# Expert weights of a mixture-of-experts layer laid out by partition, one 3 MB load per expert

## The chip, the cores and the metric

The kernel runs on one core of one Trainium2 chip. The metric is the device time of one execution in microseconds (us): the median of three runs. All data is fp32.

## The reference, cut to what matters

One encoder layer over 768 tokens of 1024 features (a prompt of 256 tokens and a sample of 512). Attention of two kinds, an output projection and a residual come first. Then each token is normalised, goes to one group of experts and to the top two of the eight experts in it; there are 32 experts, each a gated MLP with 256 hidden features. The change lies in this last part:

```python
h = rmsnorm(x, ffn_norm)                      # (tokens, 1024)
gates = ...                                   # top-1 group, top-2 experts in it
for e in range(32):
    y = (silu(h @ w_gate[e]) * (h @ w_up[e])) @ w_down[e]   # 1024 -> 256 -> 1024
    out = out + gates[:, e:e+1] * y
return rmsnorm(x + out, final_norm)
```

Each of the three weights of an expert has 1 MB, so the experts read 96 MB from HBM in all.

## The kernel before, in words

The engines run programs of their own (blocks `sync`, `gpsimd`, `scalar`, `vector`, `tensor`) that meet at semaphores. Attention (up to about 370 us) and the output projection with the router (to about 477 us) come first.

**Routing.** For each of the six tiles of 128 tokens VectorE (DVE) computes the normalised rows `h2` (`ffn_norm`, L1259) and the experts; GpSimd (POOL) stores the rows to HBM (L723) and scatters the numbers of the token-expert pairs into a table by expert (`note_pairs`, L717). `h2` is written with its features permuted: word (c, p) of the row is feature p * 8 + c, because chunk c of the transposed rows has to meet the rows p * 8 + c of the weights.

**The expert stage.** An expert works on blocks of 64 rows; `extras` gives how many further blocks it has (8 over all experts here: experts 8, 9, 14, 15 and 19 have one and expert 13 has three). The 32 experts go in groups of six, with ring slot s for the s-th expert of a group. For each expert:

- SyncE (SP), `load_expert` (L538): three loads of 1 MB, `w_gate`, `w_up` (L557) and `w_down` (L561), into one ring slot of 6144 words a partition. From the second group on it first waits until the expert six before is done (`last_done`, L554), and each load is paced: it waits for the landing of the load three issues before it (`paced`, L550). `w_gate` and `w_up` lie in SBUF as (p, c, n): partition p holds the rows p * 8 + c, so that a partition reads 8 KB in one piece. The last expert's weights go into the place of the residual, early. After the last load SP reloads the residual (L595).
- GpSimd gathers the block's rows from HBM (`gather`, L739 and L741), four experts ahead; further blocks have one buffer, and the gather of the next one waits until TensorE has transposed the one before (`e_xeT_psum`). Results are scattered to HBM (L749, and L832 for the last four).
- TensorE (PE), `pe_group` (L1810): waits for gate and up of the expert; `gate_up` (L1758) is 8 chunks times two halves of the hidden features, the halves in the two column halves of the array, each product 256 columns wide (128 of gate, 128 of up). Half h takes the hidden features 2n + h, every second word of a weight row. Then the next expert's rows are transposed (L1754), then, after a wait for `w_down` (`down_weights`, L1805), the down products of the expert before (L1773), and the transposed hidden block (L1803). The trace has two records for each fp32 product: 32 for a `gate_up`.
- ScalarE (ACT) computes the silu (L1021) and copies the results out (L1029, L1037), DVE multiplies (L1401) and copies transposed blocks (L1406, L1424, L1411).

After the last expert the rows come back from HBM (L601, L603), are weighted and added to the residual on PE (L1869) and DVE (L1448 to L1458), and stored.

Two definitions that the prediction counts with:

```python
SLOT_W = 3 * D * FF // P        # 6144 words a partition, 3 MB a slot
ring = [arena[:, a:a + SLOT_W] for a in [QKV0 + s * SLOT_W for s in range(4)] + [R0, W0]]
```

Of the kernel before, what the change touches and what calls it, by code (L numbers as in the profile page):

```python
# [18 lines left out]
P = 128  # L19
# [120 lines left out]
def build(nc, A):  # L140
# [12 lines left out]
    with ExitStack() as ctx:  # L153
# [260 lines left out]
        last_loaded = sem("last_loaded")  # L414
        gate_loaded = [sem(f"gate_loaded{s}") for s in range(RING)]
        up_loaded = [sem(f"up_loaded{s}") for s in range(RING)]
        down_loaded = [sem(f"down_loaded{s}") for s in range(RING)]
        id_ready = sem("id_ready")
# [75 lines left out]
        def _(sp):  # L494
# [43 lines left out]
            def load_expert(g, s):  # L538


                e = g * RING + s
                w = weights(g, s)
                last = is_last(g, s)
                later = not isinstance(g, int) or g > 0 and not last

                def paced(what, slot, back):
                    if later:
                        turn = g + (slot - back) // RING + 1
                        sp.wait_ge(what[(slot - back) % RING], 16 * turn)
                        sp.sem_inc(waited, 1)  # L550

                if later:
                    sp.wait_ge(last_done, e - RING + 1)
                    sp.sem_inc(waited, 1)  # L554
                for i, (n, pace) in enumerate((("w_gate", (down_loaded, s, 2)), ("w_up", (gate_loaded, s, 1)))):
                    paced(*pace)
                    sp.dma_start(w[:, i * 2048:(i + 1) * 2048],  # L557
                                 A[n][0, bass.ds(e, 1), :, :].rearrange("o (p c) n -> p (o c n)", c=DC)
                                 ).then_inc(last_loaded if last else (gate_loaded, up_loaded)[i][s], 16)
                paced(up_loaded, s, 1)  # L560
                sp.dma_start(w[:, 4096:6144],  # L561
                             A["w_down"][0, bass.ds(e, 1), :, :].rearrange("o (p j) n -> p (o j n)", p=P)
                             ).then_inc(last_loaded if last else down_loaded[s], 16)

# [514 lines left out]
        def _(dve):  # L1079
# [171 lines left out]
            def ffn_norm(t):  # L1251
                dve.wait_ge(rms2_ready, t + 1)
                link(dve.reciprocal(rs[:, t:t + 1], rs[:, t:t + 1]))
                if t == 0:
                    dve.wait_ge(gffn_in, 16)
                if t >= 2:
                    dve.wait_ge(h2_stored[t % 2], 16 * (t // 2))

                dve.scalar_tensor_tensor(h2[t % 2].rearrange("n (c p) -> n c p", c=DC),  # L1259
                                         x_tok[:, t, :].rearrange("n (p c) -> n c p", c=DC), rs[:, t:t + 1],  # L1260
                                         gain_ffn.rearrange("n (p c) -> n c p", c=DC), ALU.mult, ALU.mult).then_inc(h2_ready, 1)

# [214 lines left out]
        def _(pe):  # L1477
# [280 lines left out]
            def gate_up(b, i, w):  # L1758


                w = w[:, 0:4096].rearrange("p (g c n h) -> p g c h n", g=2, c=DC, h=2)
                for c in range(DC):
                    for h in range(2):
                        last = nc.tensor.matmul(bank(b)[h * SLOTS:(h + 1) * SLOTS, 0:2 * P].rearrange("p (g n) -> p g n", g=2),  # L1764
                                                x_eT[i][:, c, :], w[:, :, c, h, :],
                                                start=(c == 0), stop=(c == DC - 1))
                return last
# [36 lines left out]

            def down_weights(g, s):  # L1805

                if not is_last(g, s):
                    await_count(down_loaded[s % RING], 16 * (g + s // RING + 1))

            def pe_group(g):  # L1810
                words = load_counts(pe, g)
                for s in members(g):
# [3 lines left out]
                    if is_last(g, s):  # L1816
                        pe.wait_ge(last_loaded, 48)
                    else:
                        pe.wait_ge(gate_loaded[s], 16 * (g + 1))
                        pe.wait_ge(up_loaded[s], 16 * (g + 1))  # L1820
                    pe.wait_ge(xeT_ready, e + 1)
# [3 lines left out]
                    if not isinstance(g, int) or e:  # L1825
                        down_weights(g, s - 1)
                        down_before(k, g, s - 1, last_done)
                    h_transpose(k)
                    with pe.If(n > 0):
                        down_weights(g, s)  # L1830
                        with pe.Fori(0, n) as j:
                            transpose_further(before + j)
                            pe.wait_ge(hT_ready, k + j + 1)
                            pe.wait_ge(y_out, k + j + 1)
                            down(weights(g, s), 0)
                            pe.wait_ge(e_xeT, before + j + 1)
                            gate_up(1, 2, weights(g, s)).then_inc(gu_done, 1)
                            down(weights(g, s), 1).then_inc(part_done, 1)
                            h_transpose(k + j + 1)
# [78 lines left out]
```

## Time and profile before

| | us |
|---|---|
| median of 3 runs (798.39, 800.14, 801.2) | 800.14 |
| the profiled execution | 800.14 |
| its span, first to last instruction | 798.4 |
| PE busy in it | 745.3 (93%) |
| DVE, ACT, POOL busy | 301.8, 220.0, 199.4 |
| moved by DMA | 154.64 MB, 203 GB/s of HBM traffic over the span |
| mean granted TensorE clock | 0.975 of 2.4 GHz |

The sum of busy times says little here, since attention, projection and expert stage have different limits; the rows below are by stretch. The profiled execution's time stands 1.7 us over its span. In the profile "released by issue" means that an engine waited for nothing that the trace shows. A busy PE need not be a fast PE: ends of matmuls are modelled.

### The profile page before, as it was taken

To read this page: it belongs to the slowest core of one execution; us is meant where nothing else is said; L and a number is where in the kernel's file an instruction comes from. 1 tells how busy PE (TensorE), PEld (TensorE's weight loads), DVE (VectorE), ACT (ScalarE), POOL (GpSimd) and SP (SyncE) were. 2 spreads that over 40 slices of the span, in tenths; PEclk is the share of its full clock that TensorE was granted. 3 is DMA by queue.
4 is the path that set the end of the run, shared out by engine and by line. 5 is a ranking of instruction groups with operands and counts; after the bars stand their busy time and mean duration, and the time that the engine had idled before them with its cause. 6 is when DMAs were issued, how large, how long until landed. Compare 5 with 4: busy or idle time off the path is not lost. (4 is left out here: it accounts for less than half of the span.)

```text
span 798.4 us, 12355 instructions
## 1 busy us (share of the span) xinstructions
PE 745.3 (93%) x4034; PEld 411.0 (51%) x4035; DVE 301.8 (38%) x811; ACT 220.0 (28%) x595; POOL 199.4 (25%) x479
## 2 busy tenths in 40 slices
PE   8999999999888999989999974999998999999995
PEld 4555554444355666664555552555544454545542
DVE  3442211010288888980555562111111121211126
ACT  3543220111277767660211110111110111111123
POOL 1233422210023232032001223441321434342110
PEclk9999999999999999999999986999998999999999
DMA  9603002000320000000891258899999999999948
GB/s 348 258 1 106 0 1 105 1 0 1 113 104 1 2 1 1 2 1 0 347 421 76 80 213 307 273 351 372 374 344 388 391 348 333 410 379 387 401 163 347
DMA packets 36887, 154.64 MB, mean 194 GB/s; under 512 B 9674, under 2 KB 10826, under 8 KB 23904
## 3 DMA queue, kind: packets, MB, share of 16 engines
q1 hardware_dynamic: 28112, 136.50, 44.9%
q0 software_dynamic: 7648, 15.75, 6.0%
q10 hardware_dynamic: 1072, 1.70, 0.6%
q8 instruction: 28, 0.46, 0.2%
q14 instruction: 27, 0.22, 0.1%
HBM read 142.29 MB, written 20.03 MB: 203 GB/s over the span
## 5 line engine op out<-in xcount | busy, mean ns | idle before, releaser
L1499 PE MATMUL banks<-arena 128*128 128x512 f32 (+1 forms) x384 | 163.7, 580 | 2.3 <-issue 1.9
L1764 PE MATMUL banks<-arena 128*64 128x256 f32 x1280 | 158.2, 399 | 4.6 <-issue 2.4
L1764 PEld LDWEIGHTS banks<-arena 128*64 128x64 f32 x1280 | 90.9, 138 | 63.9 <-issue 10.8
L1499 PEld LDWEIGHTS banks<-arena 128*128 128x128 f32 x384 | 72.1, 193 | 79.6 <-issue 79.6
L1655 PE MATMUL banks<-arena 128*128 128x512 f32 x192 | 86.4, 598 | 1.1 <-DVE arena L1237 1.1
L1773 PE MATMUL banks<-arena 128*64 128x512 f32 x320 | 79.8, 610 | 0.5 <-ACT arena L1029 0.5
L1401 DVE TENSOR_TENSOR arena<-arena,banks 128x128 f32<-128x128 f32 x40 | 11.6, 290 | 165.4 <-ACT arena L1021 165.4
L1193 DVE TENSOR_REDUCE arena<-banks 128x1 f32<-128x512 f32 (+1 forms) x96 | 55.3, 599 | 48.0 <-PE banks L1571 41.5
L952 ACT ACTIVATE arena<-banks,arena 128x512 f32<-128x512 f32 (+1 forms) x96 | 58.3, 613 | 42.4 <-DVE arena L1196 21.0
L1021 ACT ACTIVATE arena<-banks 128x128 f32<-128x128 f32 x40 | 11.1, 278 | 160.5 <-PE banks L1764 160.5
L1655 PEld LDWEIGHTS banks<-arena 128*128 128x128 f32 x192 | 35.2, 191 | 38.8 <-issue 37.4
L741 POOL DMA_INDIRECT arena<-h_rows,arena x40 | 39.1, 977 | 34.8 <-POOL arena L739 34.8
L881 ACT ACTIVATE arena<-banks,arena 128x512 f32<-128x512 f32 (+1 forms) x24 | 16.0, 666 | 106.5 <-PE banks L1499 106.5
L1606 PE MATMUL banks<-arena 128*128 128x128 f32 x240 | 36.1, 282 | 9.0 <-issue 5.5
L749 POOL DMA_INDIRECT pair_rows<-arena x36 | 36.5, 1013 | 31.8 <-POOL arena L747 30.6
L1754 PE MATMUL banks<-arena 64*128 64x64 f32 x320 | 29.1, 233 | 15.5 <-DMA arena<-h_rows,arena 15.4
L1606 PEld LDWEIGHTS banks<-arena 128*128 128x128 f32 x240 | 26.1, 142 | 31.3 <-issue 26.2
L1571 PE MATMUL banks<-arena 96*128 96x512 f32 (+1 forms) x96 | 40.1, 540 | 2.1 <-ACT arena L952 1.2
L480 POOL TENSOR_SCALAR arena<-arena 128x2 f32<-128x2 f32 (+1 forms) x8 | 1.6, 195 | 152.6 <-ACT arena L980 152.6
L1029 ACT ACTIVATE arena<-banks 128x512 f32<-128x512 f32 x32 | 19.1, 597 | 71.7 <-PE banks L1773 71.7
L1754 PEld LDWEIGHTS banks<-arena 64*128 64x128 f32 x320 | 23.7, 142 | 29.5 <-issue 18.3
L630 POOL TENSOR_TENSOR arena<-arena 128x64 f32<-128x64 f32 (+2 forms) x24 | 8.0, 331 | 117.8 <-ACT arena L881 67.8
(201 smaller groups left out, 880.6 us busy)
## 6 DMA issues: line engine op xcount, KB each, us to landing
arena<-w_gate SPq DMA_DIRECT2D x32, 1024.0 KB, 12.3
arena<-w_up SPq DMA_DIRECT2D x32, 1024.0 KB, 12.9
arena<-w_down SPq DMA_DIRECT2D x32, 1024.0 KB, 13.3
arena<-w_in SPq DMA_DIRECT2D x3, 2048.0 KB, 8.3
arena<-pair_rows SPq DMA_DIRECT2D x5, 1024.0 KB, 11.3
arena<-w_out SPq DMA_DIRECT2D x1, 4096.0 KB, 13.1
arena<-x SPq DMA_DIRECT2D x6, 512.0 KB, 10.6
h_rows<-arena POOLq DMA_DIRECT2D x6, 512.0 KB, 5.6
```

Of the source, the lines that this page charges most:

```text
L741: pool.indirect_dma_start(x_rows[i], None, h2_dram, bass.IndirectOffsetOnAxis(ap=id_cur[0:SLOTS, i:i + 1], axis=0), bounds_check=T - 1, oo ...
L749: pool.indirect_dma_start(y_dram, bass.IndirectOffsetOnAxis(ap=yid_cur[:, i:i + 1], axis=0), y_sb[i], None, bounds_check=4 * T - 1, oob_is ...
L952: act.activation(p_tok[u % 3][:, a, 0:nt * P], bank(2 * (u % 2) + a)[:, 0:nt * P], ACT.Exp, bias=nbias[:, u % 4, a:a + 1], scale=MLA_SCALE ...
L1029: act.activation(y_sb[s % YBUF], bank(4), ACT.Copy).then_inc(y_out, 1)
L1193: dve.reduce_max(mx[:, u % 4, a:a + 1], bank(2 * (u % 2) + a)[:, 0:nt * P], X_).then_inc(dve_chain, 1)
L1499: last = nc.tensor.matmul(bank(mm % 2)[:, 0:GROUP_COLS[g]], xgT[:, t, c, :], w[:, c, :], start=(c == 0), stop=(c == DC - 1))
L1571: nc.tensor.matmul(bank(2 * (u % 2) + a)[:, 0:nt * P], qT[0:QK, 2 * j + a, tok], kT[0:QK, 2 * j + a, keys], start=True, stop=True).then_in ...
L1606: last = nc.tensor.transpose(bank(4 + tau % 2)[:, kt * P:(kt + 1) * P], p_tok[u % 3][:, a, kt * P:(kt + 1) * P], ident)
L1655: last = nc.tensor.matmul(bank(2 * (t % 2) + h), aT[:, c, t * P:(t + 1) * P], w_out_sb[:, c, h * 512:(h + 1) * 512], start=(c == 0), stop= ...
L1754: last = nc.tensor.transpose(bank(b)[:, c * SLOTS:(c + 1) * SLOTS], x_rows[i][:, c * P:(c + 1) * P], ident[half, half])
L1764: last = nc.tensor.matmul(bank(b)[h * SLOTS:(h + 1) * SLOTS, 0:2 * P].rearrange("p (g n) -> p g n", g=2), x_eT[i][:, c, :], w[:, :, c, h, ...
L1773: last = nc.tensor.matmul(bank(4)[h * SLOTS:(h + 1) * SLOTS, :], h_T[:, j * SLOTS:(j + 1) * SLOTS], w[:, j, h * 512:(h + 1) * 512], start= ...
```

## The change

On the host the three weights of an expert are laid side by side by partition: partition p of `w_expert[e]` holds gate rows c * 128 + p for c = 0..7, then up rows likewise, then down rows j * 128 + p for j = 0, 1: 24 KB in one piece, 3 MB an expert. SP loads an expert with one DMA on one semaphore per slot, and each load waits for the landing of the expert's load two before it (and for its slot). PE waits for all three weights before `gate_up`, and the later waits for `w_down` are gone. The half h of the hidden features is now h * 128 + n, 128 adjacent words, and the rows `h2` are written in their natural order.

```diff
@@ -412,9 +412,7 @@
         waited = sem("waited")
 
         last_loaded = sem("last_loaded")
-        gate_loaded = [sem(f"gate_loaded{s}") for s in range(RING)]
-        up_loaded = [sem(f"up_loaded{s}") for s in range(RING)]
-        down_loaded = [sem(f"down_loaded{s}") for s in range(RING)]
+        weights_in = [sem(f"weights_in{s}") for s in range(RING)]
         id_ready = sem("id_ready")
         rows_in = [sem(f"rows_in{i}") for i in range(RING + 1)]
         xeT_psum = sem("xeT_psum")
@@ -543,24 +541,13 @@
                 last = is_last(g, s)
                 later = not isinstance(g, int) or g > 0 and not last
 
-                def paced(what, slot, back):
-                    if later:
-                        turn = g + (slot - back) // RING + 1
-                        sp.wait_ge(what[(slot - back) % RING], 16 * turn)
-                        sp.sem_inc(waited, 1)
-
                 if later:
                     sp.wait_ge(last_done, e - RING + 1)
                     sp.sem_inc(waited, 1)
-                for i, (n, pace) in enumerate((("w_gate", (down_loaded, s, 2)), ("w_up", (gate_loaded, s, 1)))):
-                    paced(*pace)
-                    sp.dma_start(w[:, i * 2048:(i + 1) * 2048],
-                                 A[n][0, bass.ds(e, 1), :, :].rearrange("o (p c) n -> p (o c n)", c=DC)
-                                 ).then_inc(last_loaded if last else (gate_loaded, up_loaded)[i][s], 16)
-                paced(up_loaded, s, 1)
-                sp.dma_start(w[:, 4096:6144],
-                             A["w_down"][0, bass.ds(e, 1), :, :].rearrange("o (p j) n -> p (o j n)", p=P)
-                             ).then_inc(last_loaded if last else down_loaded[s], 16)
+                    sp.wait_ge(weights_in[(s - 2) % RING], 16 * (g + (s - 2) // RING + 1))
+                    sp.sem_inc(waited, 1)
+                sp.dma_start(w, A["w_expert"][bass.ds(e, 1), :, :].rearrange("o p n -> p (o n)")
+                             ).then_inc(last_loaded if last else weights_in[s], 16)
 
             sp.wait_ge(pv_done, N_UNITS)
             for s in range(4):
@@ -1256,9 +1243,7 @@
                 if t >= 2:
                     dve.wait_ge(h2_stored[t % 2], 16 * (t // 2))
 
-                dve.scalar_tensor_tensor(h2[t % 2].rearrange("n (c p) -> n c p", c=DC),
-                                         x_tok[:, t, :].rearrange("n (p c) -> n c p", c=DC), rs[:, t:t + 1],
-                                         gain_ffn.rearrange("n (p c) -> n c p", c=DC), ALU.mult, ALU.mult).then_inc(h2_ready, 1)
+                dve.scalar_tensor_tensor(h2[t % 2], x_tok[:, t, :], rs[:, t:t + 1], gain_ffn, ALU.mult, ALU.mult).then_inc(h2_ready, 1)
 
             def first_max(key, values, rev, m):
 
@@ -1758,11 +1743,11 @@
             def gate_up(b, i, w):
 
 
-                w = w[:, 0:4096].rearrange("p (g c n h) -> p g c h n", g=2, c=DC, h=2)
+                w = w[:, 0:4096].rearrange("p (g c n) -> p g c n", g=2, c=DC)
                 for c in range(DC):
                     for h in range(2):
                         last = nc.tensor.matmul(bank(b)[h * SLOTS:(h + 1) * SLOTS, 0:2 * P].rearrange("p (g n) -> p g n", g=2),
-                                                x_eT[i][:, c, :], w[:, :, c, h, :],
+                                                x_eT[i][:, c, :], w[:, :, c, h * P:(h + 1) * P],
                                                 start=(c == 0), stop=(c == DC - 1))
                 return last
 
@@ -1801,11 +1786,6 @@
 
                 pe.wait_ge(h_ready, k + 1)
                 nc.tensor.transpose(bank(3)[:, 0:P], h_tok, ident).then_inc(hT_psum, 1)
-
-            def down_weights(g, s):
-
-                if not is_last(g, s):
-                    await_count(down_loaded[s % RING], 16 * (g + s // RING + 1))
 
             def pe_group(g):
                 words = load_counts(pe, g)
@@ -1814,20 +1794,17 @@
                     n, before = extras(words, s)
                     k = e + before
                     if is_last(g, s):
-                        pe.wait_ge(last_loaded, 48)
+                        pe.wait_ge(last_loaded, 16)
                     else:
-                        pe.wait_ge(gate_loaded[s], 16 * (g + 1))
-                        pe.wait_ge(up_loaded[s], 16 * (g + 1))
+                        pe.wait_ge(weights_in[s], 16 * (g + 1))
                     pe.wait_ge(xeT_ready, e + 1)
                     gate_up(1, s % 2, weights(g, s)).then_inc(gu_done, 1)
                     if not isinstance(g, int) or e + 1 < NE:
                         transpose_rows(g, s + 1)
                     if not isinstance(g, int) or e:
-                        down_weights(g, s - 1)
                         down_before(k, g, s - 1, last_done)
                     h_transpose(k)
                     with pe.If(n > 0):
-                        down_weights(g, s)
                         with pe.Fori(0, n) as j:
                             transpose_further(before + j)
                             pe.wait_ge(hT_ready, k + j + 1)
@@ -1909,6 +1886,13 @@
     for n in WEIGHTS:
         arrays[n] = np.ascontiguousarray(np.asarray(inputs[n]))
     arrays["w_in"] = arrays["w_in"].reshape(D, -1)
+
+    def by_partition(w):
+
+        return np.ascontiguousarray(w.reshape(NE, w.shape[1] // P, P, -1).transpose(0, 2, 1, 3).reshape(NE, P, -1))
+
+    arrays["w_expert"] = np.ascontiguousarray(np.concatenate(
+        [by_partition(arrays.pop(n)[0]) for n in ("w_gate", "w_up", "w_down")], axis=2))
     A = {n: nc.dram_tensor(n, a.shape, mybir.dt.from_np(a.dtype), kind="ExternalInput").ap() for n, a in arrays.items()}
     for n, s in (("y_prompt", S_PROMPT), ("y_sample", S_SAMPLE)):
         A[n] = nc.dram_tensor(n, (1, s, D), mybir.dt.float32, kind="ExternalOutput").ap()
```

## Rows read from the trace of the kernel before

**Rows 1.** The page, section 1: busy us (share of the span) and instructions.

```profile
PE 745.3 (93%) x4034; PEld 411.0 (51%) x4035; DVE 301.8 (38%) x811; ACT 220.0 (28%) x595; POOL 199.4 (25%) x479
```

**Rows 2.** Stretches: engines' busy us (records), granted clock, DMA share, GB/s.

```profile
390.00:418.00 28.00, 28.00 (x104) 15.46 (x103) 13.98 (x61) 5.01 (x14) 0.60 (x1) 1.00 1.01 422
...
531.00:592.00 61.00, 59.91 (x448) 30.62 (x450) 11.78 (x28) 8.47 (x19) 20.09 (x34) 1.00 1.02 368
...
592.00:645.00 53.00, 47.84 (x341) 25.12 (x337) 8.63 (x20) 5.54 (x14) 16.01 (x28) 0.94 1.02 373
...
665.00:748.00 83.00, 81.71 (x614) 43.08 (x616) 15.48 (x37) 10.73 (x25) 29.02 (x50) 1.00 1.01 385
```

**Rows 3.** Groups of the page: the gate and up products (busy us, mean ns).

```profile
L1764 PE MATMUL banks<-arena 128*64 128x256 f32 x1280 | 158.2, 399 | 4.6 <-issue 2.4
```

**Rows 4.** Timeline of PE: start us, length us, line; one attention burst, three expert bursts.

```profile
333.71 1.10 PE L1625 MATMUL banks<-arena 128*64 128x128 f32 x16
...
751.64 3.87 PE L1764 MATMUL banks<-arena 128*64 128x256 f32 x32
...
756.08 1.94 PE L1773 MATMUL banks<-arena 128*64 128x512 f32 x8
...
758.21 3.88 PE L1764 MATMUL banks<-arena 128*64 128x256 f32 x32
```

**Rows 5.** SP's waits between 480 and 770 us: us in total, times, longest.

```profile
SPq L550 <- DMA arena<-w_up: 57.8, 23, 3.9
...
SPq L550 <- DMA arena<-w_gate: 53.3, 19, 4.5
...
SPq L554 <- PE banks L1773: 47.1, 10, 11.1
```

**Rows 6.** Timeline of SP, 380 to 798 us: issues of expert loads.

```profile
578.34 0.33 SPq L561 DMA_DIRECT2D arena<-w_down  x1
...
658.33 0.33 SPq L557 DMA_DIRECT2D arena<-w_gate  x1
...
743.07 0.33 SPq L561 DMA_DIRECT2D arena<-w_down  x1
```

**Rows 7.** DMA issues between 573 and 580 us: median us to landing (one w_down).

```profile
arena<-w_down SPq DMA_DIRECT2D x1, 1024.0 KB, 14.3
```

**Rows 8.** Timeline of PE around experts 13 and 14.

```profile
591.44 3.88 PE L1764 MATMUL banks<-arena 128*64 128x256 f32 x32
...
608.08 1.08 PE L1754 MATMUL banks<-arena 64*128 64x64 f32 x8 [3.54 <-DMA arena<-h_rows,arena]
...
632.11 0.68 PE L1754 MATMUL banks<-arena 64*128 64x64 f32 x8 [1.41 <-DMA arena<-h_rows,arena]
```

**Rows 9.** DMA issues between 737.5 and 744 us (one w_down).

```profile
arena<-w_down SPq DMA_DIRECT2D x1, 1024.0 KB, 11.0
```

**Rows 10.** Timeline, 469 to 489 us: last FFN norm, its store, the first transposes.

```profile
469.21 2.06 DVE L1259 SCALAR_TENSOR_TENSOR arena<-arena 128x1024 f32<-128x1024 f32 x1
...
471.57 0.58 POOL L723 DMA_DIRECT2D h_rows<-arena  x1 [12.25 <-DVE arena L1259]
...
480.35 0.18 POOL L739 COPY arena<-arena 64x1 uint32<-64x1 uint32 x1 [3.13 <-DMA h_rows<-arena]
...
488.12 1.12 PE L1754 MATMUL banks<-arena 64*128 64x64 f32 x8 [10.43 <-DMA arena<-h_rows,arena]
```

**Rows 11.** Groups of DVE: the same operation on 1024 contiguous words.

```profile
L1451 DVE SCALAR_TENSOR_TENSOR arena<-arena 128x1024 f32<-128x1024 f32 x3 | 3.9, 1285 | 0.3 <-DMA arena<-pair_rows 0.2
```

**Rows 12.** DMA issues: all gathers, then windows at 610.5, 752.5 and 767.9 us.

```profile
arena<-h_rows,arena POOLq DMA_INDIRECT x40, 7.9
...
arena<-h_rows,arena POOLq DMA_INDIRECT x1, 6.7
...
pair_rows<-arena POOLq DMA_INDIRECT x1, 6.8
...
pair_rows<-arena POOLq DMA_INDIRECT x1, 2.3
```


## The prediction

> **What bounds the kernel now.** I read the page first, then the stretches, the matmul bursts, SP's waits and single landings. The change touches the last third alone, the expert stage from the first gather (481 us) to the last product (765 us). On the page PE is busy 93% of the span [rows 1], and a reader could stop there. The table of stretches shows more [rows 2]: from 531 to 592 and from 665 to 748 us PE is busy 98% of the time **and** the 16 DMA engines are busy without a break (share 1.01 to 1.02). Both run at their limit, and what a faster PE gains has to be paid for by weights that arrive sooner.
>
> PE: an expert's gate and up products are one burst of 32 records, 40 bursts in all (32 experts and 8 further blocks of 64 rows), 158.2 us together [rows 3], and a plain expert takes 6.57 us from burst to burst (751.64 to 758.21 [rows 4]). Loads: in the expert stage SP waited 57.8 + 53.3 us for the load three issues back, and 47.1 us for a free ring slot [rows 5]. So there are two regimes. Where SP waits for a slot, PE is ahead of nothing and the loads are early; where it waits for landings, the stream of weights sets the pace and the lead of the ring melts. It melts twice. Expert 13's w_down is issued at 578.34 and takes 14.3 us, to 592.6 [rows 6, 7]; its burst starts at 591.44 [rows 8]. Expert 30's w_down is issued at 743.07 and takes 11.0 us, to 754.1 [rows 6, 9]; its burst starts at 751.64 [rows 4]. PE waits for neither today, because down is needed some 4 us after gate and up.
>
> **The change part by part**, as shifts against today (minus is earlier); bursts before expert 13: 15, before the end: 40.
>
> *FFN norm (DVE, L1259).* Both reads go with stride 8 now and take 2.06 us [rows 10]; the same operation on 1024 contiguous words takes 1.285 [rows 11]. Minus 0.8 us each. The first five lie beside PE's output products and cost nothing today; if that cover were gone they would give 5 x 0.8 = 4.0. The sixth is followed by the store of the rows (471.57), the wait for it (to 480.35), the gather and the first transposes at 488.12, for which PE waited 10.43 us [rows 10]. Taken: -0.8; other end 0, as the store lands behind two experts' loads anyway.
>
> *Gate and up products.* Same count, same columns; only the moving operand changes from every second word to 128 adjacent ones, twice. A burst now takes 3.87 us. Less the last record (0.39) and a longer first step (0.05) that leaves 3.43 for 15 steps, 229 ns each. The down products, the same two column halves with contiguous words, take 1.94 for 4 steps of 512 columns [rows 4]: less 0.59 and 0.05, 1.30 over 3 is 433, or 217 for 256 columns. If adjacent words bring the first to the second, a burst loses 15 x 12 = 0.18 us. L1625, two column halves at 128 contiguous columns, says otherwise: 1.10 less 0.27 and 0.05 over 7 steps is 111, or 223 for 256 columns [rows 4], which leaves 0.09. I take 0.18, from the row with the same operand buffer; ends 0 and 0.2. If PE bound everywhere, that would be 40 x 0.18 = -7.2.
>
> *One wait for 3 MB (PE).* Before each burst PE now waits for down too. What stands behind that wait on PE is the next expert's transposes, the down products of the expert before, and with them last_done, which frees the slot for SP, and ACT's copy and POOL's scatter. At the landings of today the wait would cost 592.6 - 591.44 = 1.2 us at expert 13 and 754.1 - 751.64 = 2.4 us at expert 30. The waits and semaphore increments that go from PE and SP (two of three DMA issues of 0.33 us per expert, and the paces) lie beside busy engines: 0. SP is never late for its own sake. The reload of the residual stays queued behind the last load, as now. POOL's order is untouched.
>
> *The stream.* Same bytes, rows of 24 KB in place of 8 KB, and up to 6 MB asked for ahead in place of 3. The engines are never idle in the full stretches, so the deeper queue gives nothing. Larger rows can save at most what separates 385 GB/s (beside gathers and scatters) from 422 (weights alone, 390 to 418 us) [rows 2], 9%; at 422 the same 8 KB rows run already, so most of the gap belongs to the other traffic, not to row starts. Taken 2%, an estimate near the lower end; ends 0 and 9%.
>
> *Gathers and scatters* share the engines with the larger rows. Under load a gather takes 7.9 us in the median and a scatter 6.8; with nothing beside it a scatter lands in 2.3 [rows 12]. PE feels it in three places: twice in the series of further blocks of expert 13, where each gather starts only after the last block's transposes (wait 3.54 at 608.08, the next one tight), and once at expert 14 (1.41) [rows 8]. Taken: 0.3 us each for one 24 KB row in the way instead of one of 8 KB, +0.9 in all; ends 0 and 15 (below).
>
> **The sum.** Stream to expert 13: starts 0.8 + 2 x 0.18 = 1.2 earlier, runs 87 us (505 to 592.6) and saves 2%, 1.7: all landed at 589.7. PE alone would be there at 591.44 - 0.8 - 15 x 0.18 = 587.9, so it waits 1.8 us and starts 1.7 earlier than now. To the last load that waits for a slot before the final full stretch (658.33 [rows 6]) about five bursts count that no gather hides: -0.9, so -2.6. The final chain of loads, 96 us, saves 1.9: expert 30 complete at 754.1 - 2.6 - 1.9 = 749.6, against a burst at 751.64: -2.0. Two last bursts, -0.4; gathers, +0.9. Total **-1.5 us**. The profiled execution is 800.14 us (span 798.4 and 1.7 around it), which is also the median of the three: **798.6 us**. Seven microseconds of PE work are taken out and most is swallowed by the stream.
>
> **Rivals.**
> *The stream gets faster (0.20).* If 24 KB rows suffer less from the interleaved gathers and close most of the 9%, PE stays the bound: -0.8, and 0.18 for each of 37 bursts that no gather hides, 6.7: 792.6 us. For it: the gap exists. Against it: 8 KB rows alone reach 422.
>
> *The gathers wait for their turn (0.20), the slower side.* Price: loaded less idle latency is about 4.5 us now. If a gather must let a whole load's share of an engine pass, that share grows from 64 KB (2.5 us at 422/16 GB/s) to 192 KB (7.5 us): +5 at each of the three places, 813; at +3, 807. It decides from about +1.6 us each on. For it: expert 13's series has no slack. Against it: the scatter of 752.9 us ran beside 4 KB rows of the residual and took 6.8 us, and the gather of 610.6 us beside 8 KB rows took 6.7 [rows 12]; doubling the row did nothing. The Trainium skill has this as a rule (DMA: Bandwidth & Descriptors, section on queues, rings and completion order): an engine changes queue only when a whole packet of many descriptors is drained. These rows neither show nor exclude it.
>
> *Stride costs nothing on PE (0.15).* The excess of 12 ns a step may belong to the column halves, as L1625 suggests. Then PE starts expert 13 only 0.8 earlier, expert 30 is complete at 754.1 - 0.8 - 1.9 = 751.4, -0.2, gathers +0.9: 800.8 us. The Trainium skill (SBUF — State Buffer, the section on Door 1) says so: two hits in each 16-byte line give full bandwidth, and every second fp32 word has just two. The burst rows speak against it with 229 to 217, L1625 half for it.
>
> *The forecast (0.45)*; if the 24 KB rows were cut up again on the way, its 2% would go and it would stand some 2 us later.
>
> **How the numbers follow.** 0.3% is 2.4 us, about what a measurement of this kernel can tell from no change. Faster: 0.20 and a third of the forecast's case, 0.36. Same: the rest of it and the stride case, 0.41. Slower: most of the gather case and a rest, 0.23. Range 791.5 to 807: from PE-bound with 0.2 a burst to gathers 3 us later each. The forecast's own range is 796.5 to 801.5.
>
> **What would show it.** L1764's group falls from 158.2 to about 151 us busy, and a burst from 3.87 to 3.69; L1259 to 1.28 us. PE waits for w_expert at expert 13 (1.8 us) and at the last one or two (under 2 us each), too short for the clock to fall: after 1.41 us of waiting the clock held, while the stretch with 3.54 shows 0.94 [rows 2, 8]. The DMA share stays at 1.0 with 385 to 393 GB/s, the median gather under 8.5 us. I am wrong if a gather's median is over 10 us (slower case), if the full stretches run above 405 GB/s (faster case), or if the burst stays at 3.87.

## The result: 7% slower, and the profile after

| | us (runs) | ratio to before, 95% interval |
|---|---|---|
| before | 799.61 (798.39 to 801.20, 4) | |
| the changed kernel | 856.27 (854.74 to 856.59, 4) | 1.0704 [1.0679, 1.0728] |

The forecast was 798.6 us with a range to 807; even the slower rival (813) is passed by 43 us. The profiled execution has a span of 853.0 us against 798.4, so 54.6 us more, and the last gate and up burst ends at 815.5 instead of 762.1: 53.4 us are lost inside the expert stage.

The page of the changed kernel, four groups of section 5 (L1749 is gate and up, L1758 the down products, L1739 the transposes of gathered rows, L1016 ACT's copy of the results; columns as in [rows 3]):

```profile
L1749 PE MATMUL banks<-arena 128*64 128x256 f32 x1280 | 152.0, 392 | 4.7 <-issue 1.9
...
L1758 PE MATMUL banks<-arena 128*64 128x512 f32 x320 | 91.3, 688 | 16.2 <-ACT arena L1016 16.1
...
L1739 PE MATMUL banks<-arena 64*128 64x64 f32 x320 | 30.2, 239 | 50.2 <-DMA arena<-h_rows,arena 50.0
...
L1016 ACT ACTIVATE arena<-banks 128x512 f32<-128x512 f32 x32 | 19.1, 597 | 139.5 <-DMA pair_rows<-arena 98.7
```

The product that was to get faster did: 158.2 [rows 3] became 152.0. What is new stands in the last column. PE waited 50.0 us for gathered rows (15.4 before) and 16.1 us for ACT's copies (0.5 before), and ACT in turn waited 98.7 us for scatters to free its buffers (3.0 before). Together PE waits 50 us more. The down products take 11.5 us more (91.3 against 79.8) for the same work, which is the clock, below; the transposes 1.1 more; the bursts 6.2 less. The sum, 50.2 + 11.5 + 1.1 - 6.2 = 56.6, is within 2 us of the 54.6.

The stretches that [rows 2] showed:

```profile
390.00:418.00 28.00, 28.00 (x110) 15.80 (x108) 12.64 (x52) 4.54 (x12) 1.14 (x2) 1.00 0.94 399
531.00:592.00 61.00, 40.41 (x261) 19.94 (x259) 6.80 (x16) 4.76 (x11) 10.64 (x18) 0.80 0.90 325
...
665.00:748.00 83.00, 72.03 (x545) 38.67 (x545) 14.07 (x34) 9.12 (x22) 27.55 (x48) 0.94 0.87 323
```

From 531 to 592 us PE falls from 98% busy to 66%, and its granted clock from 1.00 to 0.80 (a mean over time at 2.4 and at 1.2 GHz). The DMA engines, full before, are at 0.87 to 0.90. That is an average of two states: in the first 44 us of the stretch they are full (the queue view below, 90.3% and 10.2%), then weights pause, and from 645 to 655 us none move at all (share 3%). Over the whole stretch neither PE nor the DMA engines are at their limit: the kernel has lost its overlap. SP's waits (480 to 820 us) say the same from the other side, since weights are now early:

```profile
SPq L546 <- PE banks L1758: 229.6, 25, 42.0
```

SP waits 229.6 us for a free slot (47.1 before [rows 5]) and PE waits for w_expert not once. One place in detail, PE and then POOL from 539 to 576 us (start us, length us, engine, line; in brackets the idle time before and its releaser):

```profile
539.39 3.74 PE L1749 MATMUL banks<-arena 128*64 128x256 f32 x32
543.06 0.71 PE L1739 MATMUL banks<-arena 64*128 64x64 f32 x8
546.27 3.60 PE L1758 MATMUL banks<-arena 128*64 128x512 f32 x8 [2.50 <-ACT arena L1016]
...
550.06 3.67 PE L1749 MATMUL banks<-arena 128*64 128x256 f32 x32
...
573.20 1.08 PE L1739 MATMUL banks<-arena 64*128 64x64 f32 x8 [13.10 <-DMA arena<-h_rows,arena]
...
575.97 4.20 PE L1749 MATMUL banks<-arena 128*64 128x256 f32 x32
```

```profile
539.08 0.97 POOL L728 DMA_INDIRECT arena<-h_rows,arena  x1 [0.85 <-POOL arena L726]
...
574.53 0.18 POOL L726 COPY arena<-arena 64x1 uint32 x1 [25.98 <-PE banks L1739]
```

The gather that expert 8's further block needs was issued at 539.08. Its rows were transposed at 573.20, 34 us later; under load a gather took 7.9 before [rows 12]. POOL had issued it in good time and then stood still for 26 us. Bursts come 10.7 us apart here (539.39 to 550.06), where a plain expert took 6.57 before [rows 4] and takes 6.4 with the shorter product (the last two bursts of this trace start at 805.45 and 811.82). The down products that follow the wait take 3.60 us, and full speed is 1.94 [rows 4]; the granted clock is at its lower level from 546.4 to 549.8 us.

The view of DMA queues shows why. Software is GpSimd's queue (gathers, scatters), hardware is SP's (weights). A packet is one record of a transfer on one DMA engine. The columns are packets, MB and share of 16 engines. The changed kernel from 531 to 575 us:

```profile
q1 hardware_dynamic: 666, 14.40, 90.3%
q0 software_dynamic: 666, 1.49, 10.2%
```

The kernel before, same stretch:

```profile
q1 hardware_dynamic: 1905, 13.87, 85.7%
q0 software_dynamic: 880, 2.11, 15.2%
```

**666 against 666.** A weight packet here is one row of 24 KB (586 of them) or the 4 bytes with which an engine signals the end of a load (80): an engine's part of a 3 MB load is eight rows and one such signal. For each packet of the weights' queue one of GpSimd's queue was served. The counts show the ratio; the order on a single engine is not in them, so "a turn" below means one packet of each. In 44 us an engine had 666 / 16 = 41.6 turns, so one per **1.06 us**. The DMA engines are full in both views and move about the same in all (15.94 MB against 16.07), but GpSimd's queue gets less of it. Before, with 8 KB rows, there were two weight packets for each software packet (a row is served more often, and that queue had turns to spare).

How many turns does an execution (one block of 64 rows) need? Counted in the trace of the kernel of e4 below, after 505 us, by size of packet:

```
software queue: 4096 B x2851, 4 B x2023, 8 B x1002, 2052 B x44; together 5920 = 37 x 160
```

That is 160 packets for 37 of the 40 executions, 10 on each of 16 engines: five for a gather (four rows of 4 KB and one for the semaphore) and five for a scatter. (By their sizes and numbers the 4 B packets are semaphores and rows of a gather that are out of range, and the 8 B and 2052 B ones hold rows of a scatter that are.) Ten turns at 1.06 us are 10.6 us, and PE needs 6.4 us for an execution. The pace of 10.6 holds only while the weights' queue is full: PE falls behind, slots stay occupied, SP has nothing to issue, and in the pause GpSimd's queue catches up (575 to 595 us: 164 packets of weights, 466 of GpSimd's). This became theory T.

### The profile page after: what moved, and what is told of

Same layout as the page of the kernel before. It is cut to its first block and busy times, and to the rows that moved or that the text cites. A ratio compares the mean times of both kernels' runs of the same rounds, so it can differ in the third digit from the quotient of the medians.

```text
span 853.0 us, 12128 instructions
## 1 busy us (share of the span) xinstructions
PE 750.4 (88%) x4034; PEld 415.2 (49%) x4035; DVE 296.7 (35%) x811; ACT 219.7 (26%) x595; POOL 200.2 (23%) x479
## 5 line engine op out<-in xcount | busy, mean ns | idle before, releaser
L1749 PE MATMUL banks<-arena 128*64 128x256 f32 x1280 | 152.0, 392 | 4.7 <-issue 1.9
L1749 PEld LDWEIGHTS banks<-arena 128*64 128x64 f32 x1280 | 93.2, 141 | 58.7 <-issue 12.8
L1758 PE MATMUL banks<-arena 128*64 128x512 f32 x320 | 91.3, 688 | 16.2 <-ACT arena L1016 16.1
L1739 PE MATMUL banks<-arena 64*128 64x64 f32 x320 | 30.2, 239 | 50.2 <-DMA arena<-h_rows,arena 50.0
L1739 PEld LDWEIGHTS banks<-arena 64*128 64x128 f32 x320 | 24.6, 147 | 63.6 <-issue 51.2
L1016 ACT ACTIVATE arena<-banks 128x512 f32<-128x512 f32 x32 | 19.1, 597 | 139.5 <-DMA pair_rows<-arena 98.7
L1758 PEld LDWEIGHTS banks<-arena 128*64 128x64 f32 x320 | 22.2, 149 | 41.8 <-issue 37.5
```

What stands on the lines that cost most here:

```text
L1016: act.activation(y_sb[s % YBUF], bank(4), ACT.Copy).then_inc(y_out, 1)
L1739: last = nc.tensor.transpose(bank(b)[:, c * SLOTS:(c + 1) * SLOTS], x_rows[i][:, c * P:(c + 1) * P], ident[half, half])
L1758: last = nc.tensor.matmul(bank(4)[h * SLOTS:(h + 1) * SLOTS, :], h_T[:, j * SLOTS:(j + 1) * SLOTS], w[:, j, h * 512:(h + 1) * 512], start= ...
```

## The experiments

Theory T (turns): GpSimd's queue gets one packet for each row of the weights' queue while that one is full, so the length of a row sets the rate of gathers and scatters. Rival D (depth): what hurts is 6 MB asked for ahead, or one DMA of 3 MB. In the expectations of e1 to e4 I had put the turns of an execution at 14, from a count of rows; by the packets there are 10. A difference of 2 to 3 us between two experiments is not clear of noise where one of them has 2 runs. The ratios of e1 to e4 share 19 runs of the kernel before (median 799.37), those of e5 to e8 17 runs (799.67), e9 has 3 (797.38).

### e1: the changed kernel with rows of 8 KB, still one load of 3 MB

```diff
-                sp.dma_start(w, A["w_expert"][bass.ds(e, 1), :, :].rearrange("o p n -> p (o n)")
+                sp.dma_start(w.rearrange("p (k n) -> p k n", k=3),
+                             A["w_expert"][bass.ds(e, 1), :, :, :].rearrange("o k p n -> p (o k) n")
```

The host array is (expert, k, partition, words), so only the length of a piece in HBM changes.

> The changed kernel with one edit: an expert's 3 MB still come in one load, paced in the same way, but in HBM they lie as three blocks, so that each row that the load reads and writes has 8 KB, not 24. Theory T (turns): the gathers and scatters of POOL's queue get one packet for each row of the weights' queue on the same engine, so their rate is set by the row length; with 8 KB rows a turn is about 0.35 us again and the time is 792 to 800 us, gathers' waits on PE under 8 us. Rival D (depth): what delays them is that 6 MB are asked for ahead, or that a load is 3 MB in one; then nothing changes: 850 us or more.

Measured: **803.36 us** (801.10 to 807.92, 10 runs), ratio 1.0052 [1.0031, 1.0073]. PE's longest sums of waits from 470 to 830 us:

```profile
PE banks L1740 <- DMA arena<-h_rows,arena: 16.3, 4, 10.7
PE banks L1750 <- DMA arena<-w_expert: 10.2, 6, 3.8
```

53 of the 57 us are gone by the length of the row alone. The waits for gathers are back at 16.3 (15.4 before). D falls as the main cause. The expectation was too low all the same: 803.36 lies over its 792 to 800, and its "under 8 us" for the gathers' waits had overlooked that the first gather alone is 10.4 before and 10.7 here. What is left in the trace is the wait for 3 MB that the prediction spoke of. Its place was named, its size was not: at expert 13 PE waited 3.79 us, not 1.8, and the burst after it ran slow, 5.36 us:

```profile
592.16 5.36 PE L1750 MATMUL banks<-arena 128*64 128x256 f32 x32 [3.79 <-DMA arena<-w_expert]
```

### e2: rows of 12 KB

As e1 with `k=2`.

> As the one before with two blocks in HBM, rows of 12 KB. T: an execution asks of each engine for about 14 turns (4 gather rows, 8 scatter rows, 2 semaphores), 0.54 us each, 7.5 us against 6.4 us of PE work: somewhat over what PE needs, 800 to 825 us. D: 850 us or more.

Measured: **805.73 us** (804.70 to 806.77, 2 runs), ratio 1.0068 [1.0043, 1.0092]. Queues from 531 to 545 us:

```profile
q1 hardware_dynamic: 341, 3.99, 84.0%
q0 software_dynamic: 341, 0.71, 16.0%
```

Again one to one, and a turn is now 14 x 16 / 341 = 0.66 us. Ten turns are 6.6 us, hardly over the 6.4 of an execution. The window is one where both queues are full; over 531 to 575 us there are 1133 packets of weights to 945. So 12 KB sits near the boundary. It costs 2.4 us over 8 KB, which is not clear of noise (the intervals overlap), where 24 KB costs 53: not a straight slope, but a loss that sets in somewhere above 12 KB.

### e3: rows of 24 KB, one load ahead in place of two

```diff
-                    sp.wait_ge(weights_in[(s - 2) % RING], 16 * (g + (s - 2) // RING + 1))
+                    sp.wait_ge(weights_in[(s - 1) % RING], 16 * (g + (s - 1) // RING + 1))
```

> The changed kernel with one edit: an expert's load waits for the landing of the load just before it, so that 3 MB at most are on their way, as in the kernel before; rows of 24 KB. T: turns are as long as in the changed kernel, and only the short pauses between loads help POOL's queue: 825 to 855 us, PE still waits over 20 us for gathers. D: 800 to 810 us.

Measured: **844.24 us** (841.76 to 846.72, 2 runs), ratio 1.0549 [1.0507, 1.0590]. PE's waits:

```profile
PE banks L1749 <- DMA arena<-w_expert: 35.5, 12, 7.0
PE banks L1739 <- DMA arena<-h_rows,arena: 14.7, 2, 11.9
```

The queues from 531 to 575 us:

```profile
q1 hardware_dynamic: 518, 11.55, 70.3%
q0 software_dynamic: 835, 2.07, 15.1%
```

The time is as T said, and D's 800 to 810 is out, but half of the expectation failed in an instructive way. Most of the time stays lost by another wait. Each load is issued after the last one has landed, so the weights' queue runs empty in between, and there the gathers catch up (835 packets against 518). Beyond the first gather PE waits only 2.8 us more for them. It waits for weights instead, whose stream has lost a fifth (11.55 MB in 44 us against 14.40). The one-to-one ratio is there only while the other queue is full.

### e4: the compute part alone

Three loads of 1 MB with 8 KB rows, semaphores and paces as before; the weights of each kind laid out by partition, adjacent columns and `h2` in natural order as in the change.

```diff
-                w = w[:, 0:4096].rearrange("p (g c n h) -> p g c h n", g=2, c=DC, h=2)
+                w = w[:, 0:4096].rearrange("p (g c n) -> p g c n", g=2, c=DC)
...
-                                                x_eT[i][:, c, :], w[:, :, c, h, :],
+                                                x_eT[i][:, c, :], w[:, :, c, h * P:(h + 1) * P],
```

> The kernel before with the changed kernel's column order alone: weights laid out by partition, 128 adjacent columns for each half, plain FFN norm, but three loads of 1 MB with 8 KB rows, their paces and PE's later wait for w_down as before. The compute part of the change alone. T and D both: bursts of 3.67 us in place of 3.87, and of the 40 x 0.2 = 8 us of PE work some is lost to the stream of weights: 792 to 798 us.

Measured: **799.38 us** (798.44 to 802.71, 10 runs), ratio 1.0003 [0.9985, 1.0021]. The group of gate and up, PE's wait for gathers, one stretch, and one of the last bursts:

```profile
L1762 PE MATMUL banks<-arena 128*64 128x256 f32 x1280 | 149.6, 387 | 12.7 <-DMA arena<-w_up 8.5
```

```profile
PE banks L1752 <- DMA arena<-h_rows,arena: 16.4, 3, 11.3
```

```profile
665.00:748.00 83.00, 77.64 (x594) 41.94 (x590) 15.35 (x37) 10.51 (x24) 26.20 (x44) 1.00 1.00 376
```

```profile
734.24 3.67 PE L1762 MATMUL banks<-arena 128*64 128x256 f32 x32 [1.94 <-DMA arena<-w_up]
```

The expectation (792 to 798) took too little for the stream. This is the prediction's first half, shown by itself. PE's products take 8.6 us less (158.2 to 149.6), PE waits 8.5 us for w_up where it waited for none, and the time does not move. The stream moves no more than before (376 GB/s against 385), at a share of 1.00.

### e5: the load part alone

The changed kernel with the order of columns and of `h2` as before.

> The load part of the change alone: one load of 3 MB with rows of 24 KB, two loads ahead, as in the changed kernel; columns of gate and up stay alternating, the rows h2 stay permuted. Theory T (GpSimd's queue gets one packet for each row that the weights' queue sends on a DMA engine, so rows of 24 KB make its gathers and scatters take longer than an expert's products): the slower products change nothing, since PE waits for the gathers and scatters: 853 to 860 us, burst 3.87 us, some 60 us of PE's waits for gathers and for ACT's copies (which wait for scatters). Rival A (the new order of columns costs something of its own, by the clock or in the rows' layout): 845 us or less.

Measured: **851.90 us** (851.14 to 852.66, 2 runs), ratio 1.0654 [1.0625, 1.0684]. PE's waits, and the queues from 531 to 570 us:

```profile
PE banks L1741 <- DMA arena<-h_rows,arena: 46.0, 5, 12.3
PE banks L1760 <- ACT arena L1016: 11.3, 6, 3.2
```

```profile
q1 hardware_dynamic: 585, 12.80, 89.9%
q0 software_dynamic: 586, 1.29, 9.8%
```

The loss is in the load part, and rival A (845 or less) is out. The bursts here take 3.88 us and those of the changed kernel 3.67, and yet the burst of expert 8's further block starts at 575.83 against 575.97 and the last one at 810.64 against 811.82: speed of PE is worth nothing where turns set the pace. One miss: 851.9 lies below the 853 expected, and below the changed kernel by 4.4 us. PE waits 9 us less here (57.3 against 66.1); its gate and up products take 9.9 more (161.9 against 152.0), but the down products 5.3 less (86.0 against 91.3), since fewer of them fall into the lower clock (mean 0.953 against 0.948). That makes about 4 us; the two profiled executions are 2.2 apart. Why the slower product leaves PE with fewer waits stays open.

Gathers of this kernel have landings in the trace (in the changed kernel most are missing). DMA issues from 505 to 760 us, first e5, then the kernel before:

```profile
arena<-h_rows,arena POOLq DMA_INDIRECT x33, 13.0
```

```profile
arena<-h_rows,arena POOLq DMA_INDIRECT x34, 8.0
```

### e6: the kernel of e4 with rows of 4 KB

> The kernel of e4 with every load of 1 MB cut into rows of 4 KB. Theory T: half the length of a row is half the time of a turn of GpSimd's queue, so a gather under load takes 5 to 6 us in place of 8, and PE's waits for gathers behind further blocks fall under 2 us in all; twice as many rows may cost the stream some per cent (fewer GB/s than 376 at share 1.0), which PE would see as waits for w_up. 797 to 804 us, 799 if both balance. Rival (row length has no effect under 8 KB, since the gather is bound by its own 40 KB and its start): gathers unchanged, 799 to 803.

Measured: **799.13 us** (796.55 to 801.75, 10 runs), ratio 0.9996 [0.9980, 1.0012]. DMA issues from 505 to 760 us, and the queues from 531 to 575 us:

```profile
arena<-h_rows,arena POOLq DMA_INDIRECT x32, 7.1
```

```profile
q1 hardware_dynamic: 3686, 14.21, 86.7%
q0 software_dynamic: 873, 2.18, 15.0%
```

Gathers get quicker, 7.1 us against 8.0 in the kernel before (e4's landings are not in its trace), less than the 5 to 6 expected, and PE's waits behind the first gather are still 3.9 us, not under 2; the stream loses nothing (14.21 MB in 44 us, e4 has 13.69); the time stays. Far from the boundary the length of a row is of no account. It matters little for the bandwidth either: in the stretch from 390 to 418 us, weights alone, rows of 4, 8 and 24 KB move 412, 422 to 423 and 425 GB/s (e6; before and e4; e5). The changed kernel's 399 there stands at a share of 0.94, which is 424 at a full one.

### e7: the sixth expert's weights asked for later

The kernel of e4 with the three loads of the sixth expert behind the table of ids.

```diff
             load_expert(0, 4)
-            load_expert(0, 5)
             store_residual(NT - 1)
...
+            load_expert(0, 5)
             load_expert(NGRP - 1, members(NGRP - 1)[-1])
```

> The kernel of e4 with the sixth expert's three loads issued after the table of ids has come back and ahead of the last expert's, so that the store of the last tile's rows and the first gather (471 to 488 us) are not queued beside 3 MB of weights. Theory T: store and first gather take less, the first burst starts 3 to 7 us earlier; the stream of weights sets the pace at the end, and the sixth expert has to be in by its burst (about 515 us), so 793 to 799 us. Rival (the whole is bound by the stream of weights, which loses those 3 MB of early work): 799 to 804.

Measured: **805.93 us** (803.56 to 808.36, 6 runs), ratio 1.0077 [1.0055, 1.0100]. PE's waits, and two bursts:

```profile
PE banks L1762 <- DMA arena<-w_up: 12.0, 6, 4.5
```

```profile
486.46 5.81 PE L1762 MATMUL banks<-arena 128*64 128x256 f32 x30 [0.88 <-DVE arena L1431]
...
547.20 6.37 PE L1762 MATMUL banks<-arena 128*64 128x256 f32 x32 [4.52 <-DMA arena<-w_up]
```

The first burst does start 2.3 us earlier (486.46 against 488.79 in e4). 60 us on, PE stands 4.52 us for w_up, and its next burst takes 6.37 us in place of 3.67. The rival, the stream that can't do without 3 MB of early work, takes it, and by more than it said.

### e8 and e9: five more turns for each scatter, and the control

e8 adds to the kernel of e4, behind each scatter of the rows, a second one with all targets out of range:

```diff
+                pool.indirect_dma_start(y_dram, bass.IndirectOffsetOnAxis(ap=none_id, axis=0), y_sb[i],
+                                        None, bounds_check=4 * T - 1, oob_is_err=False).then_inc(y_stored[i], 16)
```

> The kernel of e4 with a second scatter behind each scatter, all of whose 128 targets are out of range, so that it moves no byte; the result is the same. Theory T, if out-of-range rows still take their packet in the queue: 9 more turns at 0.35 us on each engine, so some 23 turns or 8 us an execution against 6.4 us of products: 820 us or more, with waits of ACT for the scatter two executions back. Rival B (the price goes by the bytes that gathers and scatters move): within 3 us of e4, 798 to 803. If out-of-range rows are dropped before they become packets, T gives the same as B, and a look at the packets in the trace tells which.

Measured: **819.90 us** (819.05 to 820.75, 2 runs), ratio 1.0254 [1.0225, 1.0283]. Queues from 735 to 755 us, where both are full:

```profile
q1 hardware_dynamic: 898, 6.56, 86.6%
q0 software_dynamic: 871, 1.02, 15.6%
```

The time looked like a hit. An empty scatter still takes packets: from 470 to 800 us there are 9936 of them on the software queue against 6736 in e4, 3200 / (40 x 16) = 5 on each engine, not 9. With so many packets the count is nearly one to one with rows of 8 KB too, at 20 x 16 / 898 = 0.36 us a turn, and 30 x 16 / 1156 = 0.42 from 515 to 545 us (1156 to 1105). So 15 turns are 5.3 to 6.2 us, close to PE's 6.4 and not over it: by this count T does not call for 20 us. And the second scatter also keeps GpSimd busy. e9 replaces it with a copy and its wait, and no DMA:

```diff
-                await_count(ready, count)
+                await_count(ready, count * 2)
...
+                pool.tensor_copy(spare[:, i:i + 1], yids_sb[:, bass.ds(column, 1)]).then_inc(ready, 1)
+                await_count(ready, count * 2 + 1)
```

> The control to e8: the kernel of e4 with GpSimd held up by about as long behind each scatter of the rows (a copy of the ids and the wait for it, 1.1 to 1.3 us, as the second scatter took) but with no second scatter, so no further packets. Theory T (e8's 20 us come from the five further packets of each scatter on every DMA engine): within 3 us of e4, 797 to 803. Rival (they come from GpSimd, which issues each gather and scatter later): 815 us or more.

Measured: **812.20 us** (810.33 to 814.07, 2 runs), ratio 1.0180 [1.0091, 1.0269]. PE's wait, and PE at expert 13:

```profile
PE banks L1758 <- DMA arena<-h_rows,arena: 28.7, 6, 11.0
```

```profile
604.17 1.08 PE L1758 MATMUL banks<-arena 64*128 64x64 f32 x8 [6.75 <-DMA arena<-h_rows,arena]
```

My expectation (797 to 803) fell, and the rival's 815 is not reached either. GpSimd's time behind each scatter costs 12.8 us against e4: its gathers for further blocks go out later, PE waits (6.75 us at 604.17, e4 3.74) and loses clock (the burst at 606.95 takes 4.24 us). So e8 proves less than it seemed. The control is also weaker than it was meant to be: by the timelines the copy and its wait hold GpSimd for 0.9 us, the second scatter of e8 for 1.3. Of e8's 20.5 us over e4, 12.8 are GpSimd's time as e9 has it, and an estimate by the longer hold, 12.8 x 1.3 / 0.9, gives 18. What is left for the packets is 2 to 8 us, and the intervals of the two ratios overlap. That GpSimd's queue is served in turns shows in e8's counts; that its further packets cost time there is not shown.

No version beats the kernel before: e4 and e6 equal it, and I would keep three loads.

## Why the prediction was wrong

**The step that failed** is the term *Gathers and scatters*: "0.3 us each for one 24 KB row in the way instead of one of 8 KB, +0.9 in all; ends 0 and 15". e1 against the changed kernel puts the longer rows at 53 us. Three things were wrong in it.

1. It priced one row in the way of a gather, and at half of what its own rate gives (64 KB in 2.5 us, so 0.6 us for the 16 KB more). Every packet of GpSimd's queue has a row in its way, ten for an execution: 10 x (1.06 - 0.42) is 6.4 us more for an execution while the stream is full, and not 0.3.
2. It took a gather for a latency, felt in three places. It is also a queue with a throughput, which the scatters share. At 10.6 us for each 6.4 of PE the queue of GpSimd falls behind, and the delay grows to 34 us. ACT waits 98.7 us for scatters, a wait that no part of the prediction looked at. The range's end of 15 us had the same three places in it. The sign that the prediction gave for this case, a median gather over 10 us, is what the load part shows: 13.0 in e5.
3. The evidence against the rival compared a scatter beside 4 KB rows (6.8) with a gather beside 8 KB rows (6.7): two operations, one sample each, both with turns to spare. e6 against the kernel before made a better comparison, 7.1 against 8.0; even so the loss sets in only beyond it (above 12 KB), which no row of before could show. The queue view could have shown how near it was: 1905 to 880 packets and ten turns an execution were in the trace of before, and three times longer rows leave a third as many turns.

The rival "gathers wait for their turn" had the place right and the mechanism half right: not a whole load's share passes first, one row does, each time. Its 813 us rested on three places as well. The rule quoted there, from the Trainium skill (DMA: Bandwidth & Descriptors, section on queues, rings and completion order), has the engine alternate between queues by the packet. The traces agree with the alternation in their counts, with 666 to 666, 341 to 341, 586 to 585 and 871 to 898. They differ on what a packet is: it is not many descriptors of a load but one row, 24, 12 or 8 KB, to one packet of GpSimd's queue. The Trainium skill also advises to join loads into the largest transfer (SBUF — State Buffer, section on the DMA setup-cost knee). Here that costs: 803 us with one load of 3 MB in 8 KB rows, its paces and its one wait, against 799 with three of 1 MB, and 856 with longer rows.

**What held.** PE and the stream both at their limit, and PE's gain swallowed: shown by e4, 8.6 us taken out and 8.5 waited. The burst: 3.69 forecast, 3.67 measured, so the rival "stride costs nothing" falls (its rule in the Trainium skill, SBUF — State Buffer, section on Door 1, too: every second fp32 word costs (3.87 - 0.44) / 15 = 229 ns a step, adjacent words (3.67 - 0.44) / 15 = 215). The norm:

```profile
465.98 1.29 DVE L1246 SCALAR_TENSOR_TENSOR arena<-arena 128x1024 f32<-128x1024 f32 x1
```

2.06 became 1.29 us, as its row said. The first burst of e4 starts 1.3 us earlier than before (488.79 against 490.11).

**What was mis-sized.** The one wait for 3 MB: forecast 1.8 us at expert 13 and no lower clock; e1 shows 3.79 us and a burst of 5.36. e1 stands 4.0 us over e4, which differs in the wait, the size of the load and the paces; which of them costs it is not separated. "2% faster stream": rows of 24 KB move 425 GB/s alone against 422, 0.7%, and beside gathers no gain was to be seen. With these two put right and rows that leave gathers their turns, the forecast would have come near e1's 803, inside the range. The error that put the time outside it is the one above.

## What to carry to other kernels

When a long stream and small gathers or scatters share the DMA engines, count packets: (packets of the small queue for one step of work) x (time of one row of the large one, with the small packet beside it) has to stay under the time of that step. Here 10 x 0.42 us passed under 6.4, 10 x 0.66 was just over it and cost little, and 10 x 1.06 cost 7%. That is a rule from one kernel. Lengthen rows only where the bandwidth asks for it (here 8 KB had 422 of 425 GB/s), and read the queue view first: equal packet counts on two queues, in a window in which the DMA engines have no idle time, are the sign that one is being served at the other's pace. Where the engines have idle time, equal counts can be chance: in e8 from 645 to 665 us they are 724 to 721 at a share of 90%, made of halves of 373 to 471 and 351 to 250.

And an experiment that adds packets adds work to the engine that issues them; it needs a control that adds the same work alone, with its length read from the trace.

## What the runs showed of the hardware that I had not expected

- The turn: as many packets served of the software queue as of the hardware queue while both are full, a row being one packet, at rows of 24 and 12 KB and nearly so at 8 KB; a turn took 1.06, 0.66 and 0.36 to 0.42 us.
- A scatter whose rows are all out of range still takes five packets on each DMA engine (e8).
- A lower clock needs no long wait: in the changed kernel the down products took 3.60 us in place of 1.94 after 2.50 us of waiting for ACT, and 3.39 after 1.92 us (at 556.30). After 1.94 us for w_up (e4) a burst kept its 3.67. So the length of the last wait alone does not decide it.
- Work on GpSimd is not free even at 25% busy: about 0.9 us more behind each scatter cost 12.8 us (e9).
